# State rows in places of their own, and the last four weight pieces issued singly, in a one-core decoder layer on Trainium2

## The reference

```python
u = rmsnorm(x, g_mix[i]);  z = u @ w_in[i]                     # 1024 -> 4096
xc, conv_new = causal_conv(xa, conv_buf, ...)                  # state: last 3 rows of xa
ya, h_last = rg_lru(xc, h0, ...)                               # state: last h
yb, pool_new = pool_mix(xb, pool_buf, ...)                     # state: last 15 rows of xb
x = x + (sigmoid(ga) * (ya @ w_proj_a) + sigmoid(gb) * (yb @ w_proj_b)) @ w_out
x = x + moe(rmsnorm(x, g_moe), ...)                            # top 4 of 32 experts
ple = rmsnorm(p @ w_ple, g_ple_post) * sigmoid(rmsnorm(x, g_ple) @ w_ple_gate)
x = x + ple;  y = rmsnorm(x, g_final)
```

## Time and profile before

| what | value |
|---|---|
| median of 3 runs | 1224.89 us (1223.78 to 1225.55) |
| the profiled execution | 1225.06 us |
| its span | 1223.3 us |
| PE, DVE, ACT, POOL busy | 96%, 27%, 18%, 2% |
| bytes moved by DMA | 446.82 MB, mean 365 GB/s |
| chain that ended last | PE 78%, DMA 18% |

### The profile page before, as it was taken

How to read it: one execution, slowest core, us unless ns; L and a number is a source line. 1 busy time by engine, 2 the same in 40 slices (tenths; PEclk the granted TensorE clock), 3 DMA queues, 4 the chain that set the end, 5 groups by cost and what they waited for, 6 DMA issues and landing times.

```text
span 1223.3 us, 14451 instructions
## 1 busy us (share of the span) xinstructions
PE 1170.7 (96%) x5836; PEld 550.4 (45%) x5836; DVE 331.7 (27%) x864; ACT 221.0 (18%) x430; POOL 29.9 (2%) x65
## 2 busy tenths in 40 slices
PE   9999999999999999999989995899999999899997
PEld 7777777444343434433342442334344343334344
DVE  5744214251222213122222120132131222111223
ACT  2666301122210110101010111211101010101024
POOL 2001000000000000000000030000000000000000
PEclk9999999999999999999999998899999999899999
DMA  9936563589999999999999999599999999999951
GB/s 289 372 118 218 181 270 133 233 319 421 428 426 426 424 434 430 430 429 436 431 432 430 430 431 430 210 410 430 434 433 431 429 429 435 433 429 428 425 215 39
DMA packets 43095, 446.82 MB, mean 365 GB/s; under 512 B 7070, under 2 KB 10366, under 8 KB 27320
## 3 DMA queue, kind: packets, MB, share of 16 engines
q1 hardware_dynamic: 40288, 440.04, 86.3%
q0 software_dynamic: 2496, 5.71, 1.5%
q10 hardware_dynamic: 256, 0.30, 0.1%
HBM read 444.51 MB, written 1.88 MB: 365 GB/s over the span
## 4 chain that ended last, share of the span: by engine, by line
PE 78%; DMA 18%; ACT 1%; DVE 1%; POOL 1%; issue 1%; SPq 0%; DVEq 0%; ACTq 0%
PE ps L1234 29%; PE ps L891 16%; PE ps L1255 14%; DMA ring<-in_w_gate_up 8%; DMA ring<-in_w_down 7%; PE ps L1113 4%; PE ps L1269 4%; DMA out<-work 3%; PE ps L1043 2%; PE ps L1388 2%; PE ps L1211 2%; PE ps L1200 1%; PE ps L925 1%; POOL out L860 1%; PE ps L1105 1%; PE ps L912 1%
## 5 line engine op out<-in xcount | busy, mean ns | idle before, releaser
L1234 PE MATMUL ps<-ring,work 128*64 128x512 f32 x2000 | 441.8, 595 | 1.7 <-DMA ring<-in_w_gate_up 1.6
L1234 PEld LDWEIGHTS ps<-ring,work 128*64 128x64 f32 x2000 | 140.7, 137 | 272.0 <-issue 256.2
L1255 PE MATMUL ps<-ring,work 128*64 128x512 f32 x992 | 227.4, 607 | 16.5 <-DMA ring<-in_w_down 16.5
L891 PE MATMUL ps<-work,ring 128*128 128x288 f32 x736 | 180.6, 407 | 0.0
L891 PEld LDWEIGHTS ps<-work,ring 128*128 128x128 f32 x736 | 139.5, 190 | 39.8 <-issue 1.7
L1255 PEld LDWEIGHTS ps<-ring,work 128*64 128x64 f32 x992 | 71.8, 140 | 146.2 <-issue 141.6
L2174 DVE TENSOR_SCALAR work<-ps 128x512 f32<-128x512 f32 x32 | 22.1, 692 | 372.2 <-PE ps L1234 372.2
L2146 DVE TENSOR_TENSOR work<-ps,gain_fours 128x256 f32<-128x256 f32 x56 | 23.8, 425 | 285.2 <-PE ps L1113 285.2
L1675 ACT ACTIVATE work<-work 128x512 f32<-128x512 f32 x32 | 20.2, 631 | 426.3 <-DVE work L2174 426.3
L1113 PE MATMUL ps<-work,x_tok 128*128 128x128 f32 x512 | 62.6, 280 | 0.0
L1113 PEld LDWEIGHTS ps<-work,x_tok 128*128 128x128 f32 x512 | 59.0, 192 | 3.9 <-issue 2.1
(11 more groups left out here) (290 smaller groups left out, 675.1 us busy)
## 6 DMA issues: line engine op xcount, KB each, us to landing
ring<-in_w_gate_up SPq DMA_DIRECT2D x48, 4096.0 KB, 28.8
ring<-in_w_down SPq DMA_DIRECT2D x23, 4096.0 KB, 28.7
ring<-in_w_gate_up SPq DMA_DIRECT2D x29, 2048.0 KB, 14.0
ring<-in_w_down SPq DMA_DIRECT2D x15, 2048.0 KB, 17.8
ring<-in_w_in SPq DMA_DIRECT2D x7, 2048.0 KB, 18.5
work<-in_w_gate_up SPq DMA_DIRECT2D x3, 1536.0 KB, 12.5
ring<-in_w_proj_b SPq DMA_DIRECT2D x2, 2048.0 KB, 9.8
ring<-in_w_proj_a SPq DMA_DIRECT2D x2, 2048.0 KB, 10.2
```

The costliest lines, as they stand in the source:

```text
L891: mm = pe.matmul(out(b), lhs, rhs, start=(k == 0), stop=(k == len(pairs) - 1))
L1234: mm = pe.matmul(ps[half(g), b, :], xg[:, k, i % 2, :], dealt(blocks[2 * (k % 2) + at], g), start=False, stop=(k == KC - 1))
L1255: mm = pe.matmul(ps[half(g), b, :], hT_of[i % 2][:, 4 * j + k, :], blocks[k][:, 512 * g:512 * g + 512], start=False, stop=(4 * j + k == KC ...
```

## The change

Two things change. First, the state rows get other places: the conv and pool rows go into two blocks of 512 columns, `tail_halves` (one in `x_tok`, one in `work`), the h rows to the start of what is later `square_row`. The conv and pool stores are issued by half rows, 36 in place of 18; the two h stores go first and have a semaphore of their own. ScalarE's wait for all stores ahead of the embedding's copy is removed; a wait for the two h stores stands ahead of the squares. Second, in the last quad the last four pieces (the down pieces of the last two experts) are issued singly, the last two of them in halves, and `weigh_down` waits for each by itself.

```diff
-        state_z = flat_w[:, W:W + 2 * D].rearrange("p (i d) -> p i d", i=2)
-        state_h = flat_w[64:64 + DB + 1, W:W + D]
+        state_h = flat_w[0:DB + 1, 4 * W:4 * W + D]
+        tail_halves = [flat_x[:, 2 * D + 512:3 * D], flat_w[:, 4 * W + D + 512:4 * W + 2 * D]]
...
-        last_half_landed = sem("last_half_landed")
-        last_landed = sem("last_landed")
+        first_half_landed = [sem(f"first_half_landed{j}") for j in range(2)]
+        last_landed = [sem(f"last_landed{n}") for n in range(4)]
...
+            def last_piece(quads, at, e0):
+
+                ring_place_used(quads, at)
+                i, q = STREAM[at]
+                here, src = whole_piece((at - EXTRAS) % SLOTS), expert_rows(q, e0 + i)[:, piece_half(q)]
+                n, at_half = at - (QUAD_PIECES - 4), 0
+                if n >= 2:
+                    sp.dma_start(here[:, 0:2 * D], src[:, 0:2 * D]).then_inc(first_half_landed[n - 2], 16)
+                    at_half = 2 * D
+                sp.dma_start(here[:, at_half:4 * D], src[:, at_half:4 * D]).then_inc(last_landed[n], 16)
+
             def quad_pieces(quads, e0, last=False):
...
-                    if last and at == QUAD_PIECES - 2:
-                        ring_place_used(quads, at)
-                        sp.dma_start(whole_piece(r), expert_rows(q, e0 + i)[:, piece_half(q)]) \
-                            .then_inc(piece_landed[r], 16)
-                        ring_place_used(quads, at + 1)
-                        place_, src = whole_piece((r + 1) % SLOTS), expert_rows(q + 1, e0 + i)[:, piece_half(q + 1)]
-                        sp.dma_start(place_[:, 0:2 * D], src[:, 0:2 * D]).then_inc(last_half_landed, 16)
-                        sp.dma_start(place_[:, 2 * D:4 * D], src[:, 2 * D:4 * D]).then_inc(last_landed, 16)
+                    if last and at >= QUAD_PIECES - 4:
+                        for j in range(2):
+                            last_piece(quads, at + j, e0)
                         continue
...
-            stores = [
-                (conv_prompt[0, 0], state_z[13:16, 0, :]),
-                (pool_prompt[0, 0], state_z[1:16, 1, :]),
-                (h_prompt[0], state_h[0:1, :]),
-                (h_sample[0], state_h[1:1 + DB, :]),
-            ]
-            for b in range(DB):
-                at = 16 + DS * b
-                stores += [(conv_sample[0, b], state_z[at + 1:at + DS, 0, :]),
-                           (pool_sample[0, b, PB - DS:PB, :], state_z[at:at + DS, 1, :])]
+            pool.dma_start(h_prompt[0], state_h[0:1, :]).then_inc(h_stored, 16)
+            pool.dma_start(h_sample[0], state_h[1:1 + DB, :]).then_inc(h_stored, 16)
+            stores = []
+            for h in range(2):
+                own = slice(512 * h, 512 * h + 512)
+                conv_rows, pool_rows = (tail_halves[h][64 * i:64 * i + TAIL, :] for i in range(2))
+                stores += [(conv_prompt[0, 0, :, own], conv_rows[13:16, :]),
+                           (pool_prompt[0, 0, :, own], pool_rows[1:16, :])]
+                for b in range(DB):
+                    at = 16 + DS * b
+                    stores += [(conv_sample[0, b, :, own], conv_rows[at + 1:at + DS, :]),
+                               (pool_sample[0, b, PB - DS:PB, own], pool_rows[at:at + DS, :])]
             for dst, src in stores:
                 pool.dma_start(dst, src).then_inc(state_stored, 16)
+            pool.wait_ge(h_stored, 16 * 2)
             pool.wait_ge(state_stored, 16 * (len(stores) + 1))
...
-            def weigh_down(Q, i, j, in_halves=False):
+            def weigh_down(Q, i, j, ends=False):
...
-                if in_halves:
+                n = 2 * (i % 2) + j
+                if ends:
                     s, _ = place(Q, i, GU_PIECES + j)
                     blocks = [whole_piece(s)[:, D * k:D * k + D] for k in range(4)]
-                    pe.wait_ge(last_half_landed, 16)
+                    if n < 2:
+                        pe.wait_ge(last_landed[n], 16)
...
-                    if in_halves and k == 2:
-                        pe.wait_ge(last_landed, 16)
+                    if ends and n >= 2 and k % 2 == 0:
+                        pe.wait_ge(first_half_landed[j] if k == 0 else last_landed[n], 16)
...
                         dst = state_h[:, 512 * h:512 * h + 512] if i == 2 else \
-                            state_z[0:TAIL, i, 512 * h:512 * h + 512]
+                            tail_halves[h][64 * i:64 * i + TAIL, :]
...
-                act.wait_ge(state_stored, 16 * (5 + 2 * DB))
                 for t, h in HALVES:
                     embedded(t, h)
...
             def embedding_squares():
 
+                act.wait_ge(h_stored, 16 * 2)
                 for t in range(TT):
```

More of the change, by code:

```diff
@@ L416, in hybrid_layer @@
         state_stored = sem("state_stored")
+        h_stored = sem("h_stored")
         top_ready = sem("top_ready")
@@ L1319, in quad @@
                     begin_down(m, 0)
-                    weigh_down(Q, i, 0)
+                    weigh_down(Q, i, 0, last and j == 1)
                     turn_hidden(m, 1)
-                    weigh_down(Q, i, 1)
+                    weigh_down(Q, i, 1, last and j == 1)
                     turn_pair_weights(m)
@@ L1326, in quad @@
                     begin_down(m, 1)
-                    weigh_down(Q, i + 1, 0)
+                    weigh_down(Q, i + 1, 0, last and j == 1)
                     weigh_down(Q, i + 1, 1, last and j == 1)
```

## The result

The changed kernel takes 1205.03 us (median of 4 runs, 1204.72 to 1205.82), the kernel before 1224.61 beside it: ratio 0.9841, 95% interval 0.9824 to 0.9858, 19.6 us faster. Forecast were 1203.3, in a range of 1200.9 to 1209.5. The profiled execution took 1204.72 us (span 1202.9), 20.3 less than the one before, where 21.8 were forecast.

The account below looks back on a forecast made before the run. The prediction took the weight stream as the bound, with TensorE having 4.6 us to spare in a pair. From 1225.06 it subtracted 17.4 us of stream and 4.4 of tail: 1203.3 us, range 1200.9 to 1209.5.

Parts of the forecast that it names:

- (b): Weight stream around the embedding: earlier refills arrive before the ring drains, so the stream runs through; 17.4 us back.
- R2: Last quad gives less: clock still falls (1205.3), or ple_gate loads or last half come late (1207.7); chance 0.12.
- (a): ScalarE's embedding copy loses its store wait at cost 0; TensorE's last embedding product starts 17.9 us earlier.
- The upper bound of (b): Weight stream: from landings of the last quad's first down-weights, 1158.90 against 1139.1, at most 19.8 us can come back.
- (c): GpSimd's queue: 38 stores in place of 20, ending near 810, nobody waits for the issues; 0 added.
- (d): ScalarE ahead of the embedding's squares: new wait for two h stores, cover some 31 us, cost 0.
- R4: Embedding's squares: h stores land late, TensorE waits from 778, stream misses bytes after some 2 us; chance 0.04.
- (e): Last quad's last four weight pieces, issued singly: 2.4 us of wait and 1.9 of clock go, 4.4 in all.
- (f): TensorE's gate products in the last quad: the ple_gate loads are late next, with 0.6 us of cover.
- R1: After the gap the ring stays thin, embedding work uses up the cover; only 13.2 us back (1207.5); chance 0.12.
- R3: State-row stores take from the stream by their number, 1.1 us (1204.4); chance 0.68 together with the main forecast.
- R5: Embedding copy: the removed wait uncovers another of the same length, leaving the tail alone, 1220.7; chance 0.02.

Follow-up runs that it names:

- the 15th store: Changed kernel with ScalarE's embedding copy held until the 15th of the 36 row stores had landed: 1212.4 us.
- the 19th: Changed kernel with ScalarE's embedding copy held until the 19th of the 36 row stores had landed: 1222.1 us.
- the 13th store: Changed kernel with ScalarE's embedding copy held until the 13th of the 36 row stores had landed: 1208.9 us.
- part one alone: Changed kernel with its last four weight pieces issued as in the kernel before; state rows moved, copy without its wait: 1208.95 us, and 1209.25 when timed again.
- quarter rows: Changed kernel with conv and pool rows stored by quarter rows, 72 stores in place of 36, same bytes: 1206.53 us.

## Why the prediction was right

**The mechanism: right.** The stream's missed time sets the price, not TensorE's stall. The table shows it with five lengths of stall. The margin that (b) worked out for the fourth refill, the landing at 797.4 less the refill, is 3.7 us with the refill where it came in the end (793.74), and 3.8 us is what the experiments measured as free. That they agree so closely is in part luck: (b) also has some 1 us from a refill to its first bytes, and the 3.7 us leave it out. The time alone, 1205.0, would have fitted the 1205.3 of R2 as well; the landings and the rows of the tail decide.

**(a), the wait gone: right.** TensorE's 17.9 us went, and the refills came 1.8 us earlier still, for the clock's part that was left aside.

**(b), the size of the stream term: 17.4 forecast, 16.0 measured.** This is the term that was mis-sized. It was worked out from the mean rate of one window. The bytes of the weight queue from 690 to 900, in the kernel before and in the changed one:

```profile
q1 hardware_dynamic: 2832, 82.58, 92.3%
```

```profile
q1 hardware_dynamic: 3084, 89.82, 99.5%
```

They are 7.24 MB apart, 16.8 us at 431 GB/s. So 0.6 us of the 1.4 lies in the window: it ended at 820, and the kernel before moved 440 GB/s from 820 to 840. Another 0.3 us lies between the two traces, since the changed kernel's gate-up weights landed 0.3 us later before the gap, at 702.23 (670.69 + 31.54) where it had been 701.91. About 0.5 us is left, bytes that were missed and didn't make a landing late. Windows of 1 us ahead of the gap, in the kernel before:

```profile
765.00:766.00 1.00, 0.00 (x0) 0.00 (x0) 0.00 (x0) 0.00 (x0) 0.00 (x0) 0.50 0.92 397
766.00:767.00 1.00, 0.00 (x0) 0.00 (x0) 0.00 (x0) 0.00 (x0) 0.00 (x0) 0.50 0.69 295
...
768.00:769.00 1.00, 0.00 (x0) 0.00 (x0) 0.00 (x0) 0.00 (x0) 0.00 (x0) 0.50 0.76 328
769.00:770.00 1.00, 0.02 (x4) 0.02 (x4) 0.00 (x0) 0.66 (x2) 0.00 (x0) 0.50 0.08 33
```

The share of the engines falls to 0.7 already at 766, while the last of them works beyond 769. The same at the end of the changed kernel's stream:

```profile
1157.00:1158.00 1.00, 1.00 (x10) 0.41 (x3) 0.42 (x1) 0.06 (x1) 0.00 (x0) 1.00 0.81 332
1159.00:1160.00 1.00, 1.00 (x3) 0.38 (x2) 0.83 (x2) 0.00 (x0) 0.00 (x0) 1.00 0.60 246
1161.00:1162.00 1.00, 1.00 (x12) 1.00 (x11) 0.91 (x2) 0.43 (x3) 0.00 (x0) 1.00 0.24 98
```

The 16 engines end over 3 to 6 us. If a piece has landed only when its last engine is done, the quick engines lose more time in a gap than the slow ones, and only the slow ones' loss counts later. The excess of bytes missed over landings is there in the experiments too. From 690 to 900 the weight queue moved 85.98 MB with the 15th store and 82.25 with the 19th, which is 8.9 us against 7.4 and 17.6 against 16.7; over the four stalled kernels from the 13th store on it is 0.4 to 1.5 us. That the engines' unequal progress is the cause is argued from these windows; no row shows the engines one by one.

The upper bound of (b), 19.8 us, came from a pace that the stream doesn't hold even without a gap: in part one alone the last quad's first down pair landed at 1142.86, not at 1139.1. Where those 3.8 us go was not followed up.

**(c) and (d), stores and the new wait: right.** The 36 row stores were issued from 719.5 to 737.8, the last landed some 71 us after its issue, near 808 (810 forecast), and the h stores after 7.3 and 9.3 us, more than 30 us before the squares. R4 needed them to land after 802: issued last, they landed at 801.6, and the kernel took 1228.9, slower than before. The mechanism of that rival is real, and only the order of issue keeps it away. By its own rule, a us for each beyond 778 and 2 us of cover, a landing at 801.6 costs 21.6 us; it cost 23.9, since the clock's fall delays the refill too.

**(e), the tail: right in the profiles** (20.4 - 16.0 = 4.4), and 2.8 to 4.0 in the medians, as the clock's fall is no sure part of it. The clock's part was put at 1.9 us from two different views, 5.35 less the 3.44 of a chain; like with like it is 1.75. Of the rule that was drawn on there, the Trainium skill, "TensorE: Matmul & The Clock Gate", Part 1, which has the clock follow how busy the array was, the trace of the changed kernel shows this much: from 540 on the clock fell twice, at 740 to 750 behind matmuls of one partition (L1172, L1177) and at 1050 behind 5.01 us of idling. That a wait for weights of this length must bring a fall does not follow: the two profiles of part one alone show one wait with and one without, and the last section shows waits of equal length with both outcomes. The halves, which the transfers allowed but which nothing asked for, gave nothing.

**(f), what is late next: right, and now at its limit.** The stream's end moved by 16.0 us, TensorE's by 20.4. The w_ple_gate loads, which released GpSimd at 1163.54, land just as TensorE begins its gate products (1163.46). By these rows, more speed in the last pair would end in a wait for these loads; no run tried it.

**The rivals.** R1 (the ring thin after the gap) fell: no window lacks bytes. R2's first half, a fall of the clock at the first down piece, is in neither profile of the changed kernel; it did not foresee the fall at 1050, by which one of the two comes 1.6 us later to the last pair than the other. R3 (1.1 us for the stores) fell: without all 36 the median is 0.3 us lower and the pair lands 0.08 us earlier. R5 fell: no other wait came in its place.

**What the prediction passed over.** It gave TensorE 4.6 us to spare in each pair and took the stream as the bound up to the last quad. That held up to 1040. The 5.01 us of idling ahead of the last quad, with the lower clock behind it, use the spare time up, and from there TensorE itself is about as late as its weights.

## What to carry to other kernels

Where a stream of weights is the bound, price a stall by how late the next refill comes against the landing of what is in flight, not by the idle time of the engine that stalls. Take the gain from landings of the same piece; the mean rate of one window was off by 1.4 us here, part of it by where the window ended. Look also for the place where the engine behind the stream has nothing left to spare: from there on its own time counts, and not the stream's. And when several stores share a slow queue, the order of issue decides who waits: the two that are needed early go first.

## What the runs showed of the hardware that was not expected

The granted clock falls after some waits for a down pair and not after others of the same length. Waits of TensorE for down pieces between 540 and 1190 (us in total, times, longest), in the kernel with quarter rows and in the changed one:

```profile
PE ps L1267 <- DMA ring<-in_w_down: 15.0, 6, 2.5
```

```profile
PE ps L1267 <- DMA ring<-in_w_down: 18.4, 12, 2.5
```

The first had six waits of 2.5 us. After each of them the 16 matmuls behind it took 5.3 us, with the clock at 0.66 to 0.87 in the windows of 5 us. The second had five waits of 2.5 us and seven of 0.35 to 0.98 us, and not one fall: its 16 matmuls took 3.65 us each time. At the same place, first with quarter rows, then in the changed kernel:

```profile
614.33 5.35 PE L1267 MATMUL ps<-ring,work 128*64 128x512 f32 x16 [2.50 <-DMA ring<-in_w_down]
```

```profile
614.94 3.65 PE L1267 MATMUL ps<-ring,work 128*64 128x512 f32 x16 [2.49 <-DMA ring<-in_w_down]
```

The kernel before has both in one trace (2.51 us with a fall at 556, 2.50 without at 614). So the length of the wait does not decide it, and what does is open. Both profiled executions took nearly the same (1205.24 and 1204.72): in the midst of the stream TensorE has the time to spare, and after a fall its short wait for the second down pair is gone. A fall is paid for in the last quad, at 1050 and in the last pair.

And small stores on GpSimd's queue landed about 2 us apart, from 7.3 us after issue for the first to 71.4 for a later one, while the weight stream lost nothing to the 36 of them that could be measured.
